# A hybrid decoder layer on one core: GLA's decays as running products on VectorE, its queries and MoBA's turned through DRAM

## The reference: what is computed

```python
n = RMSNorm(h); u = n @ W_in      # q,k,v,gate and low-rank forget gate of GLA | q,k,v of MoBA
log_a = log_sigmoid(gk_lr @ w_gk_up + b_gk) / 16            # GLA's decay, per head and key channel
S_t = diag(exp(log_a_t)) S_{t-1} + k_t^T v_t ;  o_t = q_t S_t   # 4 heads, dk 64, dv 128
# MoBA, 8 heads of 64: at 256 tokens this is causal softmax attention with a bias by distance
h = h + concat(rmsnorm(o_g) * silu(g_g), o_m) @ W_out
```

## Time and profile before

| | |
|---|---|
| median of 3 runs | 529.13 us (528.93 to 530.37) |
| the profiled execution, its own time | 529.96 us |
| its span | 528.0 us (1.96 us of its time lie outside the span) |
| busy in the span | PE 516.1, PEld 419.6, DVE 329.3, ACT 274.7, POOL 91.5 us |
| granted clock of PE, mean | 0.995 |

### The profile page before, as it was taken

The page is one execution under the profiler, slowest core; times in us unless marked ns, Lnnn a source line. Parts: engine busy times, 40 slices in busy tenths (PEclk is TensorE's granted clock), DMA queues, the critical chain, the costliest instruction groups (busy, mean ns, idle before and its releaser), DMA issues.

```text
span 528.0 us, 7035 instructions
## 1 busy us (share of the span) xinstructions
PE 516.1 (98%) x2543; PEld 419.6 (79%) x2543; DVE 329.3 (62%) x436; ACT 274.7 (52%) x336; POOL 91.5 (17%) x169
## 2 busy tenths in 40 slices
PE   7999999999999999998999999999999999999994
PEld 4778888888788888876778888888888888888883
DVE  3687556565636374456997686565666556374675
ACT  4974454534435284875352865435444353452736
POOL 1504232223200110002221000222322232110000
PEclk9999999999999999999999999999999999999999
DMA  7999887786888766334459385888878867738202
GB/s 254 375 330 356 263 254 237 219 256 204 250 239 301 225 246 234 125 125 160 132 153 311 108 294 171 229 260 240 252 213 234 263 210 243 241 131 271 77 1 79
DMA packets 79464, 115.71 MB, mean 219 GB/s; under 512 B 5808, under 2 KB 51840, under 8 KB 79312
## 3 DMA queue, kind: packets, MB, share of 16 engines
q1 hardware_dynamic: 71472, 93.34, 57.0%
q0 software_dynamic: 7808, 21.99, 12.2%
q10 hardware_dynamic: 160, 0.07, 0.1%
HBM read 105.66 MB, written 11.28 MB: 221 GB/s over the span
## 4 chain that ended last, share of the span: by engine, by line
PE 92%; DVE 2%; SPq 2%; ACT 2%; DMA 1%; issue 1%; DVEq 0%; ACTq 0%
PE acc L561 86%; PE side L561 4%; SPq L439 1%; PE turn L601 1%; DMA raw<-in_ffn_w_gu 1%; PE turn L561 1%; ACT junk L932 1%; DVE w_lo L1209 0%; ACT w_hi L921 0%; DVE pr L1420 0%; SPq L429 0%; ACT L1179 0%; ACT L948 0%; DVE pr L1418 0%; DVE pr_sq L1439 0%
## 5 line engine op out<-in xcount | busy, mean ns | idle before, releaser
L1209 DVE TENSOR_TENSOR w_lo<-raw,w_hi 128x2048 fp32r<-128x2048 f32 (+1 forms) x87 | 192.6, 2216 | 104.8 <-ACT w_hi L921 104.7
L921 ACT ACTIVATE w_hi<-raw 128x2048 fp32r<-128x2048 f32 (+1 forms) x87 | 161.2, 1857 | 101.9 <-PE acc L561 99.9
L561 PE MATMUL acc<-w_hi,hT_hi 128*128 128x512 f32 x496 | 196.2, 396 | 0.2 <-DVE w_lo L1209 0.2
L561 PE MATMUL acc<-w_lo,hT_hi 128*128 128x512 f32 x496 | 193.5, 390 | 0.0
L561 PE MATMUL acc<-w_hi,hT_lo 128*128 128x512 f32 x496 | 193.4, 390 | 0.0
L561 PEld LDWEIGHTS acc<-w_hi,hT_hi 128*128 128x128 f32 x496 | 93.4, 188 | 22.2 <-issue 2.1
L561 PEld LDWEIGHTS acc<-w_hi,hT_lo 128*128 128x128 f32 x496 | 93.4, 188 | 19.8
L561 PEld LDWEIGHTS acc<-w_lo,hT_hi 128*128 128x128 f32 x496 | 93.5, 188 | 18.5
L487 POOL DMA_DIRECT2D act_in<-act_dram x92 | 50.1, 551 | 120.2 <-DMA act_dram<-act_sq 113.3
L561 PE MATMUL acc<-w_hi,a_hiT 128*128 128x512 f32 x176 | 68.6, 390 | 0.0
L561 PE MATMUL acc<-w_lo,a_hiT 128*128 128x512 f32 x176 | 68.5, 389 | 0.0
(11 more groups left out here) (170 smaller groups left out, 329.5 us busy)
## 6 DMA issues: line engine op xcount, KB each, us to landing
raw<-in_ffn_w_gu SPq DMA_DIRECT2D x82, 512.0 KB, 5.2
raw<-in_ffn_w_down SPq DMA_DIRECT2D x40, 512.0 KB, 5.3
raw<-in_w_in SPq DMA_DIRECT2D x24, 512.0 KB, 4.5
act_dram<-act_sq POOLq DMA_DIRECT2D x23, 256.0 KB, 5.5
act_in<-act_dram POOLq DMA_DIRECT2D x92, 64.0 KB, 3.6
raw<-in_w_out SPq DMA_DIRECT2D x8, 512.0 KB, 4.5
raw<-in_w_ple_gate SPq DMA_DIRECT2D x8, 512.0 KB, 5.5
raw<-in_ffn_w_gu SPq DMA_DIRECT2D x10, 256.0 KB, 6.2
```

Of the source, the lines that this page charges most:

```text
L561: return nc.tensor.matmul(o, lhsT, rhs, start=start, stop=stop, skip_group_check=True)
L921: A(w_hi[:, slot, :nk * N], raw[:, slot, :nk * N], ACT.Copy).then_inc(hi_ready, 1)
L1209: V.tensor_tensor(w_lo[:, slot, :nk * N], raw[:, slot, :nk * N], w_hi[:, slot, :nk * N].bitcast(F32), ALU.subtract).then_inc(lo_ready, 1)
```

## The change

1. **Decays.** PE turns log_a itself to channel-major (`T_a`, 4 transposes in one `turn` bank), ACT takes exp once into `prefix`. POOL sets `suffix` to ones. DVE then widens both level by level (`widen`): at each level the second half of each block's prefix products is multiplied by the last of the first half, the first half's suffix products by the product of the second half. `D0` to `D7`, the constant matrices, `la_hi` and `la_lo` go.
2. **Diagonal.** `dot` on DVE multiplies q and k token-major and sums over channels; ACT writes identity times this sum into `AT` (`dg`, 8 instructions of 128 by 128). The PE step `diag`, its copies and the clearing of `AT` go.
3. **Turning.** The order of W_in's blocks becomes GLA q and k, MoBA q, MoBA k, then v and gate as before. GLA's q and k (first) and MoBA's q (second) are turned through DRAM like `h`: DVE squares (`g_sq`, `q_sq`), POOL out and back (`nat_turn`), ACT from `back` (`T_g0`, `T_g1`, `T_q`). PE turns only MoBA's k.
4. **Layout.** `MIX`, `ACT_STEPS` and `DVE_STEPS` are written anew. The scores go to `turn` banks, `pv0` and `pv1` to `side` banks. The scaling by 1/sum goes from DVE to ACT (`nm0` to `nm3`), with two buffers `pr`. A level pair's masked copies take both halves of the heads at once. An exp table load is brought forward (`tabE`). The forget gate's inner product is padded to 128 rows.

```diff
-WIN_BLOCKS = [("q_m", Q_M), ("k_m", K_M), ("qk_g", QK_G), ("v_m", V_M), ("v_g", V_G), ("g_g", G_G)]
+WIN_BLOCKS = [("qk_g", QK_G), ("q_m", Q_M), ("k_m", K_M), ("v_m", V_M), ("v_g", V_G), ("g_g", G_G)]
...
 MIX = {
...
-    (38, 1): ["T_k0", "D0"],
-    (38, 2): ["T_k1", "D1"],
-    (38, 3): ["D2"],
...
+    (35, 0): ["lr"],
+    (35, 1): ["z"],
+    (37, 0): ["T_a"],
+    (38, 3): ["lv0"],
+    (39, 3): ["lv1"],
+    (40, 1): ["T_k0", "T_k1"],
+    (40, 3): ["lv2", "sc0.0", "sc0.1"],
+    (41, 2): ["sc1.0", "sc1.1"],
+    (42, 1): ["lv3"],
+    (42, 2): ["sc2.0", "sc2.1"],
+    (43, 1): ["sc3.0", "sc3.1"],
+    (43, 3): ["pv0"],
+    (44, 2): ["pv1"],
+    (44, 3): ["pvg0"],
...
+            def nat_turn(i):
+
+                pool.wait_ge(nat_turned, i + 1)
+                pool.dma_start(nat_dram[i], nat_sq[:]).then_inc(nat_out, 16)
+                pool.wait_ge(nat_out, 16 * (i + 1))
+                if i:
+                    pool.wait_ge(g_turned, 2)
+                for j in range(4):
+                    pool.dma_start(back[32 * j:32 * j + 32, :].rearrange("p (i e) -> p i e", i=4),
+                                   bass.AP(tensor=nat_dram.tensor, offset=i * P * 2 * N + 2 * P * j, ap=[[2 * N, 32], [64 * N, 4], [1, 2 * P]])
+                                   ).then_inc(nat_back, 16)
...
-                elif s[0] == "D":
-
-                    d = int(s[1])
-                    m, hp, half = d // 4, d // 2 % 2, d % 2
-                    o = side_open(s)
-                    pe.wait_ge(la_lo_ready, 1)
-                    lhs = slice(m * T + hp * P, m * T + (hp + 1) * P)
-                    r = seg[:, (m + 4 * half) * P:(m + 4 * half + 4) * P]
-                    mm(o, la_hi[:, lhs], r, True, False)
-                    mm(o, la_lo[:, lhs], r, False, True).then_inc(side_done, 1)
+                elif s == "T_a":
+                    t = TURN[s]
+                    turn_open(t)
+                    pe.wait_ge(la_ready, 1)
+                    for hp in range(2):
+                        for m in range(M):
+                            ins = flip(turn[:, t % 2, (2 * hp + m) * P:(2 * hp + m + 1) * P],
+                                       log_a[:, m * T + hp * P:m * T + (hp + 1) * P])
+                    ins.then_inc(turn_done, 1)
...
-                elif s == "diag":
-                    o = [side_open(f"diag.{hh}") for hh in range(2)]
-                    pe.wait_ge(turn_act, turned("T_g1"))
-                    for k in range(4):
-                        c = slice(k * P, (k + 1) * P)
-                        for hh in range(2):
-                            r = slice(64 * hh, 64 * hh + 64)
-                            ins = mm(o[hh][:, c], k_gT[r, c], q_gT[r, c], True, True)
-                            if k == 3:
-                                ins.then_inc(side_done, 1)
...
+            def turned_back(a):
+
+                act_e.wait_ge(nat_back, 64)
+                A([q_gT, k_gT][a][:].rearrange("p (k i e) -> p k i e", k=4, i=4),
+                  view(back[:], [[32, 4], [2 * P, 4], [1, 32]], P * a), ACT.Copy,
+                  scale=[GDK ** -0.5, 1.0][a]).then_inc(g_turned, 1)
...
+                elif s == "dg":
+                    act_e.wait_ge(nat_turned, 1)
+                    act_e.wait_ge(dots, M)
+                    for m in range(M):
+                        for hd in range(GH):
+                            A(AT[:, 4 * (hd % 2) + 2 * (hd // 2) + m, :], ident[:], ACT.Copy, scale=qk[:, m, hd:hd + 1]
+                              ).then_inc(diag_set, 1)
...
+            def widen(lv):
+
+
+                half, w = (1 << lv) // 2, 1 << lv
+                second, of_first = half, half - 1
+                if lv < 7:
+                    dims, one = [[w, 2 * T // w], [1, half]], [[w, 2 * T // w], [0, half]]
+                else:
+                    dims, one = [[T, 2], [1, half]], [[T, 2], [0, half]]
+                    second, of_first = P + half, P + half - 1
+                if lv > 1:
+                    dve.wait_ge(Z_ready, 2 * lv - 2)
+                link(V.tensor_tensor(view(suffix[:], dims), view(suffix[:], dims), view(prefix[:], one, w - 1), ALU.mult))
+                dve.wait_ge(Z_ready, 2 * lv - 1)
+                return mark(V.tensor_tensor(view(prefix[:], dims, second), view(prefix[:], dims, second),
+                                            view(prefix[:], one, of_first), ALU.mult))
```

More of the change, by code:

```diff
@@ L69 @@
 MIX = {
-    (35, 1): ["lr"],
-    (36, 1): ["z", "T_q0", "T_q1"],
-    (38, 1): ["T_k0", "D0"],
-    (38, 2): ["T_k1", "D1"],
-    (38, 3): ["D2"],
[L75 to L93, removed]
+    (35, 0): ["lr"],
[12 more added lines that the diff above has]
+    (44, 3): ["pvg0"],
+    (45, 1): ["pvg1"],
+    (45, 2): ["pv2"],
     (46, 0): ["pv3"],
@@ L97 @@
 }
[L100 to L108, removed]
+ACT_STEPS = ["hi38", "tabE", "nat0", "z", "hi39", "T_a", "dg", "T_g0", "T_g1", "hi40", "nat1", "hi41", "hi42", "nat2", "T_q", "T_k0", "T_k1",
+             "hi43", "sc0", "nm0", "hi44", "sc1", "nm1", "nat3", "hi45", "sc2", "nm2", "hi46", "sc3", "nm3", "pv0", "nat4", "pv1", "hi47", "pvg", "pv2", "hi48", "pv3",
+             "nat5", "groot", "hi49"]
+DVE_STEPS = ["lr", "z", "g_sq", "zmin", "lo38", "la", "dot", "lo39", "Z0", "q_sq", "lv0", "Z1", "lo40", "lv1", "Z2", "lo41",
+             "sc0", "lv2", "lo42", "rc0", "Z3", "pr0", "sc1", "lo43", "rc1", "lv3", "pr1", "sc2", "lo44", "rc2", "pr2", "sc3", "lo45", "rc3", "pr3", "pv0", "lo46", "pv1", "lo47", "pvg", "pv2", "lo48", "pv3",
              "gg", "o_g", "lo49"]
@@ L136, in plan_turns @@
         for s in MIX[at]:
-            if s[:3] in ("T_q", "T_k", "T_g"):
+            if s in ("T_a", "T_k0", "T_k1"):
                 add(s, who="act")
-            elif s[:2] == "T_" or s[:2] == "pv" and s[:3] != "pvg":
+            elif s[:2] in ("T_", "sc") or s in PV_TURN:
                 add(s)
@@ L151, in plan_side @@
 def plan_side():
-    uses = [("gain0", "dve"), ("gain", "dve"), ("bias_row", "dve")]
+    uses = ["gain0", "gain", "bias_row"]
     for at in sorted(MIX):
         for s in MIX[at]:
[L157 to L168, removed]
+            if s[:2] == "lv":
+                uses += [f"{s}.{hh}" for hh in range(2)]
+            elif s[:2] not in ("T_", "sc") and s not in PV_TURN:
+                uses.append(s)
+    return {name: (i, i + 1) for i, name in enumerate(uses)}
 TURN, TURN_AT = plan_turns()
 SIDE = plan_side()
-SIDE_AT = {i: (who, c) for i, who, c in SIDE.values()}
 def turned(name, k=0):
@@ L1053, in step @@
                     nat(int(s[3]))
-                elif s[:3] in ("T_q", "T_k", "T_g"):
+                elif s[:3] == "T_k":
                     evacuate(s)
+                elif s[:3] == "T_g":
+                    turned_back(int(s[3]))
+                elif s == "T_q":
+                    act_e.wait_ge(nat_back, 128)
+                    A(q_mT[:].rearrange("p k (m i e) -> p (k m) i e", m=M, i=4),
+                      view(back[:], [[32, 8], [2 * P, 4], [1, 32]]), ACT.Copy, scale=MD ** -0.5).then_inc(q_turned, 1)
```

324 lines of the change are left out of this document (183 added, 141 removed).

## The result

The changed kernel takes 525.76 us (median of 4 runs, 524.25 to 526.58), the kernel before 529.32 in the runs beside it (528.93 to 530.37). The ratio is 0.9926, 95% interval 0.9906 to 0.9947. The profiled execution took 525.94 us with a span of 524.1. So the change is worth 3.6 us where 7.8 were forecast, and the time lies 0.76 us above the forecast range.

The account below looks back on a forecast made before the run. PE, busy 516.1 of 528.0 us, was taken to bound the kernel. Removals of 9.8 us less waits of 1.5 and 0.5 gave 7.8, so 521.3 us against the median of 529.13; range 518.8 to 525.0.

Parts of the forecast that it names:

- What bounds the kernel, and what PE loses: PE, busy 516.1 of 528.0 us, bounds; removing D0 to D7, diag and 12 transposes gains 9.8 us.
- diag's 4.74: PE's diag visit: 3.67 us, 1.81 of it waiting for DVE, plus 1.07 of slow-clock weight matmuls, all go.
- z keeps its price: PE's z visit stays at 1.23 us although its inner side is padded from 48 to 128 rows.
- The transfer: GLA's turn through DRAM: out at 208.5, back at 217, T_g1 done at 218.1, Z0 3.1 us before PE asks.
- the estimate from the Trainium skill: Strided-copy trap: eight squares of one turn at 19 times 1.31 us, 199 us; the prediction held that the trace disagrees.
- Behind it: DVE's chain after Z0: PE waits 0.3 us at lv1 and 1.0 at unit 40, 1.3 to 1.5 in sum.
- A granted clock of 1.00 in the windows from 196 to 300: Expected sign in the profile after: PE's clock shows no fall in that stretch.
- a rival at 1.07: Second clock fall after the wait at unit 40 adds 1.07 us, giving 522.4; within the 0.19 late-first-turn-or-clock rival.
- a chance of 0.19: Rival that GLA's first turn is late, 523.0 up to 525 us, or the clock falls again, 522.4.
- I put down 0.5 us: Allowance for PE waits in the softmax stretch, where DVE runs close to PE through the score pairs and pvg0's bank.
- 2.0 in all: PE's new waits: 1.5 us at lv1 and unit 40 plus 0.5 in the softmax stretch.

Follow-up runs that it names:

- a_best2: Changed kernel with a_hold_lo40's edits and two buffers for the turned probabilities instead of one; 520.14 us, ratio to before 0.9831.
- b_nodiag: Kernel before without the diag visit's eight matmuls and the two masked copies behind them; 526.48 us, ratio to before 0.9949.
- a_hold: Changed kernel with SP holding back the weight loads of units 48, 49 and 50 until probabilities of pairs 1, 2 and 3 are back; 521.28 us.
- a_hold_lo40: Changed kernel with a_hold's held loads, DVE's lo40 and lo41 ahead of the lv0 and lv1 copies, PE's lv1 and lv2 visited later; 519.90 us.

## Why the prediction was wrong, step by step

- *What bounds the kernel, and what PE loses.* Right: 9.8 forecast, 9.9 between the profiles of before and of a_best2, 10.5 for the changed kernel's own layout. In it diag's 4.74 was right as what leaves PE's timeline and wrong as a gain by itself: b_nodiag gives 2.65, the rest being DVE's lateness, which moves on, and a fall of the clock that not every run has. "z keeps its price" was wrong in its favour: 0.86 instead of 1.23.
- *The transfer.* The size was 1 us short: back at 218.0 and not at 217, T_g1 done at 219.2 and not at 218.1. The prediction took the DMA shares of the old layout's slices 15 and 16, 6 and 3 tenths; in the new one the windows from 212 to 220 are full. It cost nothing at lv0, where 3.1 us were in hand. By the estimate from the Trainium skill (VectorE: DVE Perf Modes, The three transpose paths) eight squares would have taken 199 us; the turn took 9.6. The page ties its factor of 19 to a large innermost stride at the destination, which this transfer does not have, so the rule does not bear on it and no run here tests it.
- *Behind it.* Right in mechanism: 0.48 at lv1 instead of 0.3, 1.07 at unit 40 instead of 1.0, together 1.69 on the raster against 1.3 to 1.5. That the sizes agree so well is partly luck: the whole chain ran about 1 us late from T_g on up to q_sq (done at 223.5 instead of 222.4), while PE reached lv0 1 us early (222.2 instead of 223.2), and the copies started behind q_sq, where the forecast had them behind lv0. The copies of lv0 took 1.37 each (2.75 for two) against 1.3.
- *The clock.* "A granted clock of 1.00 in the windows from 196 to 300" was wrong: 0.57 in 232 to 236, and 1.65 us. The prediction had it as a rival at 1.07, taken from diag, and inside a chance of 0.19. The wait that it forecast itself at unit 40 brought it in two profiles and not in five.
- **The step that failed:** "I put down 0.5 us, between nothing and the 1.81 that DVE's lateness cost at diag". The stretch cost 3.8 us (1.26 at pv1, 2.38 at pv3, 0.2 at pvg0), and all but the last by waits for the probabilities' transfers, not for DVE and the banks. The step looked at what DVE does per pair and never followed the probabilities' turn to its visit in the new order. Before, pair 3 starts out at 271.63 and pv3 follows 17 us later; after, it starts at 272.91 and PE is at pv3 at 282.6, 9.7 us later. The timeline of POOL and PE in the kernel before:

```profile
271.63 0.56 POOL L507 DMA_DIRECT2D pr_dram<-pr_sq  x1 [4.28 <-DVE pr_sq L1439]
276.91 2.19 POOL L513 DMA_DIRECT2D prT<-pr_dram  x4 [4.71 <-DMA pr_dram<-pr_sq]
...
288.98 0.88 PE L561 MATMUL turn<-prT,nat 128*64 128x256 f32 x8
```

These rows say it: the transfer out took 5.3 us beside a weight load, not the 3.1 of the earlier trace rows, and the 17 us to the visit hid it. The last of the four pieces was issued at 278.5 and none took more than 4.6 us, so pair 3 was back at least 5.8 us before pv3. With GLA's part shorter and the scores later, the new layout took 7.6 us of the 17. The prediction weighed the pace of a turn under load (h's 15.2 us) for GLA's and MoBA's queries and not for the four turns of the probabilities, which fell into full windows.
- *Share of the causes.* Taking away the collisions gives 4.5 us by the medians (a_hold), of which the profiles put 3.1 on the waits at the pv visits and 1.65 on a clock that stayed whole; taking away DVE's waits gives 1.4 more (a_hold_lo40). a_hold alone lies at 521.28, where the forecast was. That agreement is partly luck: its profile loses 1.7 at lv1 and unit 40 and 0.6 at pv3 where the forecast had 2.0 in all, and it gains 0.4 at z that the forecast did not have.
